# State-space stage of a hybrid backbone on one core: the order inside a tick, the head of the stage, and who adds the two directions of the carried part

## What is computed, cut to what matters

```python
decay = jnp.exp(jnp.where(tri, la[l] - la[s], -jnp.inf))
y_diag = (cc @ bc.T * decay * dt) @ x                # inside the tile
states = bc.T @ (x * to_end)                         # what the tile adds to the state
h = h * chunk_decay + state                          # serial, from tile to tile
y_off = (cc @ h_start) * jnp.exp(la)                 # what was carried in
```

## Time and profile before

| What | us |
|---|---|
| median of 3 runs | 3817.47 |
| the profiled execution, its own time | 3822.76 |
| span of the profiled execution | 3820.9 |
| TensorE busy, share of the span | 88% |
| VectorE busy, share of the span | 63% |
| ScalarE, GpSimd busy, share of the span | 28%, 29% |
| mean granted TensorE clock | 0.953 of 2.4 GHz |

### The profile page before, as it was taken

The page is one execution under the profiler, slowest core; times in us unless marked ns, Lnnn a source line. Parts: engine busy times, 40 slices in busy tenths (PEclk is TensorE's granted clock), DMA queues, the critical chain, the costliest instruction groups (busy, mean ns, idle before and its releaser), DMA issues. The chain is left out here.

```text
span 3820.9 us, 47998 instructions
## 1 busy us (share of the span) xinstructions
PE 3354.3 (88%) x18164; PEld 2734.6 (72%) x18164; DVE 2402.0 (63%) x3949; ACT 1087.8 (28%) x1981; POOL 1093.0 (29%) x794
## 2 busy tenths in 40 slices
PE   6899999999958886886997889999999588958698
PEld 2787888888848785555783577888888488845477
DVE  4134566765448996886564324566875489968765
ACT  2112222212235554332210211222221355523321
POOL 4233334332202232211222423433443022232121
PEclk8999999999979998998998899999999799989899
DMA  5254232223172232344436155322332733133451
GB/s 197 78 150 152 75 98 92 93 87 93 56 216 68 80 96 87 112 114 151 127 99 222 52 114 177 99 85 86 106 96 74 202 92 94 44 110 112 130 152 64
DMA packets 414842, 423.30 MB, mean 111 GB/s; under 512 B 56993, under 2 KB 351393, under 8 KB 413459
## 3 DMA queue, kind: packets, MB, share of 16 engines
q1 hardware_dynamic: 368628, 315.22, 28.6%
q10 hardware_dynamic: 45984, 105.01, 7.8%
HBM read 287.76 MB, written 124.01 MB: 108 GB/s over the span
## 5 line engine op out<-in xcount | busy, mean ns | idle before, releaser
L764 PE MATMUL l_p_acc<-l_u_hi,l_w_hi 128*128 128x512 f32 (+1 forms) x2208 | 606.4, 376 | 26.7 <-ACT l_p_stg L828 12.1
L764 PE MATMUL l_p_acc<-l_u_hi,l_w_lo 128*128 128x512 f32 (+1 forms) x2208 | 588.5, 368 | 0.0
L764 PE MATMUL l_p_acc<-l_u_lo,l_w_hi 128*128 128x512 f32 (+1 forms) x2208 | 587.7, 367 | 0.0
L679 POOL TENSOR_TENSOR l_w_hi<-l_wt,l_p_zero 128x1024 fp32r<-128x1024 f32 x100 | 201.2, 2012 | 914.4 <-PE l_p_acc L764 834.6
L764 PEld LDWEIGHTS l_p_acc<-l_u_hi,l_w_hi 128*128 128x128 f32 x2208 | 384.2, 190 | 104.2 <-issue 30.6
L764 PEld LDWEIGHTS l_p_acc<-l_u_hi,l_w_lo 128*128 128x128 f32 x2208 | 381.2, 189 | 72.0
L764 PEld LDWEIGHTS l_p_acc<-l_u_lo,l_w_hi 128*128 128x128 f32 x2208 | 381.4, 189 | 71.7
L1494 PE MATMUL l_at_pS<-l_at_k_hi,l_at_q 128*128 128x512 f32 (+1 forms) x400 | 166.1, 415 | 125.6 <-ACT l_at_prob L1610 68.9
L1728 DVE TENSOR_REDUCE l_at_nmax<-l_at_pS 128x1 f32<-128x1280 f32 (+1 forms) x144 | 197.2, 1370 | 115.9 <-PE l_at_pS L1495 114.0
L681 POOL TENSOR_TENSOR l_w_lo<-l_wt,l_w_hi 128x1024 fp32r<-128x1024 f32 x100 | 265.8, 2658 | 7.8
L921 DVE TENSOR_TENSOR l_p_R<-l_p_sw,l_p_rs 128x512 f32<-128x512 f32 x72 | 49.6, 689 | 287.4 <-PE l_p_sw L743 287.4
(11 more groups left out here) (361 smaller groups left out, 7264.7 us busy)
## 6 DMA issues: line engine op xcount, KB each, us to landing
l_wt<-w_in SPq DMA_DIRECT2D x104, 512.0 KB, 3.9
l_n_wa<-w_ada SPq DMA_DIRECT2D x10, 2048.0 KB, 17.1
kf_d<-l_p_R SPq DMA_DIRECT2D x72, 256.0 KB, 4.0
xbc_d<-l_p_fin ACTq DMA_DIRECT2D x28, 640.0 KB, 3.0
l_at_K<-kf_d SPq DMA_DIRECT2D x64, 256.0 KB, 3.0
qk_d<-l_p_late ACTq DMA_DIRECT2D x12, 1280.0 KB, 4.6
l_oT<-o_d SPq DMA_DIRECT2D x10, 1024.0 KB, 6.8
l_sd_fed<-xbc_d SPq DMA_DIRECT2D x72, 128.0 KB, 2.5
```

The costliest lines, as they stand in the source:

```text
L679: pool.tensor_tensor(w_hi[m % 2][:], wt[:, m % 2], zero[:].unsqueeze(2).to_broadcast([P, KD, P]), ALU.add).then_inc(w_rounded, 1)
L764: mm = pe.matmul(acc[:, a:a + w], (w_hi, w_lo)[wp][m % 2][:, k], (u_hi, u_lo)[up][:, k, t0 + c:t0 + c + w], start=(k == n == 0), stop=(k = ...
```

## The change

Eight edits, all in `ssd_stage`:

1. In TensorE's tick the carried product comes first, ahead of the first transposes.
2. DVE no longer adds the two directions of the carried part (L2122 goes). TensorE multiplies both with the identity: two L2002 products for each half instead of one.
3. Layer 0, groups 1 to 3: one pair of steps in each of the ticks j = 1 to 9, where j = 1 had two and j = 9 none. Group 0 and layer 1 keep their pairs.
4. Where a tick of groups 1 to 3 still has two pairs (layer 1, j = 1 and j = 7), the second comes after the outputs on TensorE and after the gate on DVE.
5. ScalarE stores output n - 2 at the end of its tick, not at the start.
6. The operands of the exponents have 10 rows instead of 128. POOL sets two rows of one operand only, DVE rounds `sel` once, and one transfer copies it to the eight slots.
7. The first group is loaded in four column ranges, the context, the first and the last two latent tiles, then the rest; ScalarE issues the B rows of each, SP the x rows. The third to sixth tile wait only for their own ranges.
8. The d transfers come after the second group's load, ahead of the pairs 1 and 2, and DVE waits for them at its first gate.

```diff
-    def step_pairs(j):
-        pairs = [0, 1] if j == 1 else [j] if 2 <= j < NSTEP else []
-        if j == NO - 1:
-            pairs = list(range(j, NSTEP))
-        return [2 * k + d for k in pairs for d in range(2)]
+    def step_pairs(g, j):
+        if g and NO > NSTEP:
+            pairs = [j - 1] if j else []
+        else:
+            pairs = [0, 1] if j == 1 else [j] if 2 <= j < NSTEP else []
+            if j == NO - 1:
+                pairs = list(range(j, NSTEP))
+        return [[2 * k + d for d in range(2)] for k in pairs]
+
+    def steps_early(g, j):
+        return step_pairs(g, j)[:1] if g else step_pairs(g, j)
+
+    def steps_late(g, j):
+        return step_pairs(g, j)[1:] if g else []
...
-        seg_l = sb(nc, ctx, tag + "seg_l", [P, RING, 2, P], F32R)
-        seg_r = sb(nc, ctx, tag + "seg_r", [P, RING, 2, HPG, P], F32R)
-        sel = sb(nc, ctx, tag + "sel", [2 + 2 * HPG, HPG, P])
+        SR = 2 + 2 * HPG
+        seg_l = sb(nc, ctx, tag + "seg_l", [SR, RING, 2, P], F32R)
+        seg_r = sb(nc, ctx, tag + "seg_r", [SR, RING, 2, HPG, P], F32R)
+        sel = sb(nc, ctx, tag + "sel", [SR, HPG, P])
+        sel_r = sb(nc, ctx, tag + "sel_r", [SR, HPG, P], F32R)
...
+        first_cols = ((slice(0, CTX), xc_in), (slice(CTX, CTX + 2 * P), xm_in), (slice(T - 2 * P, T), xm_in), (slice(CTX + 2 * P, T - 2 * P), xb_in[0]))
...
-                load_group(0)
-                sp.dma_start(sel[:], sel_d).then_inc(sel_in, 16)
-                for half in range(2):
-                    with nc.allow_non_contiguous_dma(reason="one value per head"):
-                        sp.dma_start(d_s[HD * half:HD * (half + 1), :], skip.rearrange("(n b) -> b n", b=2)[half].partition_broadcast(HD)).then_inc(skip_in, 16)
+                for cols, landed in first_cols:
+                    sp.dma_start(xb[:, 0, 0:XT, cols], xbc_d[0:XG, cols].rearrange("(n p) t -> p n t", p=P)).then_inc(landed, 16)
+                    if landed is xc_in:
+                        sp.dma_start(sel[:], sel_d).then_inc(sel_in, 16)
                 sp.wait_ge(xb_in[0], 32)
+                sp.wait_ge(sel_rounded, 1)
+                sp.dma_start(seg_r[2:SR].bitcast(F32).rearrange("p r d h l -> p (r d) (h l)"),
+                             sel_r[2:SR].bitcast(F32).rearrange("p h l -> p (h l)").unsqueeze(1).to_broadcast([SR - 2, 2 * RING, HPG * P])).then_inc(sel_put, 16)
                 load_pair(0)
                 for n in range(RING):
                     load_decays(n)
                 load_group(1)
+                for half in range(2):
+                    with nc.allow_non_contiguous_dma(reason="one value per head"):
+                        sp.dma_start(d_s[HD * half:HD * (half + 1), :], skip.rearrange("(n b) -> b n", b=2)[half].partition_broadcast(HD)).then_inc(skip_in, 16)
                 load_pair(1)
                 load_pair(2)
...
-                    elif p == (0 if g else CT):
+                    elif g == 0 and p == CT:
+                        pe.wait_ge(xm_in, 64)
+                    elif p == (0 if g else CT + 4):
...
-                        pe.wait_ge(zeroed, 1)
+                        pe.wait_ge(ones, 1)
+                        pe.wait_ge(sel_put, 16)
...
-                        mm = pe.matmul(pY[:, b + t * P:b + (t + 1) * P], us[:, n % 2, 0, 2 * t:2 * t + 2].rearrange("p h e -> p (h e)"), ident[:, :],
-                                       start=False, stop=True)
+                        for d in range(2):
+                            mm = pe.matmul(pY[:, b + t * P:b + (t + 1) * P], us[:, n % 2, d, 2 * t:2 * t + 2].rearrange("p h e -> p (h e)"), ident[:, :],
+                                           start=False, stop=d == 1)
...
+                    if 0 <= n < NO * GROUPS:
+                        carried(n)
                     if todo:
                         prep(g, todo[0], max(n + 1, 0))
                     if ahead:
@@ -2017,18 +2038,23 @@
                     if len(todo) > 1:
                         prep(g, todo[1], 0)
                     preps_done += len(todo)
-                    if 0 <= n < NO * GROUPS:
-                        carried(n)
                     if g < GROUPS:
-                        for k in step_pairs(j):
-                            step(g, k)
+                        for pair in steps_early(g, j):
+                            for k in pair:
+                                step(g, k)
                     if ahead:
                         products(n + 1, preps_done)
                     if 0 <= n < NO * GROUPS:
                         outputs(n)
+                    if g < GROUPS:
+                        for pair in steps_late(g, j):
+                            for k in pair:
+                                step(g, k)
 
...
+                for cols, landed in first_cols:
+                    act.dma_start(xb[:, 0, XT, cols], xbc_d[1024:1024 + P, cols]).then_inc(landed, 16)
...
-                    if 0 <= n - 3 < NO * GROUPS:
-                        store(n - 3)
                     if todo:
                         prep(g, todo[0])
...
                         act.activation(cb[:, n % 2], pC, ACT.Copy).then_inc(cb_copied, 1)
+                    if 0 <= n - 3 < NO * GROUPS:
+                        store(n - 3)
...
-                pool.memset(seg_l[:].bitcast(F32), 1.0).then_inc(ones, 1)
-                pool.memset(seg_r[:].bitcast(F32), 0.0).then_inc(ones, 1)
+                pool.memset(seg_l[0:2].bitcast(F32), 1.0).then_inc(ones, 1)
...
                     dve.tensor_tensor(us[:, n % 2].rearrange("p d h e -> p (d h) e"), pU[:, :].rearrange("p (k e) -> p k e", e=HD),
-                                      decay.unsqueeze(2).to_broadcast([P, 2 * HPG, HD]), ALU.mult).then_inc(u_split, 1)
-                    dve.wait_ge(u_split, n + 1)
-                    dve.tensor_tensor(us[:, n % 2, 0], us[:, n % 2, 0], us[:, n % 2, 1], ALU.add).then_inc(u_scaled, 1)
+                                      decay.unsqueeze(2).to_broadcast([P, 2 * HPG, HD]), ALU.mult).then_inc(u_scaled, 1)
...
+                    else:
+                        dve.wait_ge(skip_in, 32)
...
+                        last = dve.tensor_scalar(mask[:, d, h], tri[:, d], -1.0, 1e30, ALU.add, ALU.mult)
+                last.then_inc(built, 1)
                 dve.wait_ge(sel_in, 16)
+                dve.tensor_copy(sel_r[:], sel[:]).then_inc(sel_rounded, 1)
                 dve.wait_ge(zeroed, 1)
-                dve.wait_ge(ones, 2)
-                for s in range(RING):
-                    for d in range(2):
-                        last = dve.tensor_copy(seg_r[0:2 + 2 * HPG, s, d], sel[:])
-                last.then_inc(built, 1)
-                dve.wait_ge(skip_in, 32)
...
                     if g < GROUPS:
-                        for k in step_pairs(j):
-                            step(g, k)
+                        for pair in steps_early(g, j):
+                            for k in pair:
+                                step(g, k)
                     if 0 <= n - 1 < NO * GROUPS:
                         gate(n - 1)
+                    if g < GROUPS:
+                        for pair in steps_late(g, j):
+                            for k in pair:
+                                step(g, k)
```

More of the change, by code:

```diff
@@ L1847, in ssd_stage @@
+    def steps_early(g, j):
+        return step_pairs(g, j)[:1] if g else step_pairs(g, j)
+    def steps_late(g, j):
+        return step_pairs(g, j)[1:] if g else []
     TICKS = NO * (GROUPS + 1) + 1
     RING, FEDS = 4, 3
-    with stage(nc, tag + "xc_in", tag + "xb0_in", tag + "xb1_in", tag + "o0_in", tag + "o1_in", tag + "o2_in", tag + "seg0_in", tag + "seg1_in", tag + "seg2_in", tag + "seg3_in", tag + "skip_in", tag + "sel_in",
+    with stage(nc, tag + "xc_in", tag + "xm_in", tag + "xb0_in", tag + "xb1_in", tag + "o0_in", tag + "o1_in", tag + "o2_in", tag + "seg0_in", tag + "seg1_in", tag + "seg2_in", tag + "seg3_in", tag + "skip_in", tag + "sel_in", tag + "sel_rounded", tag + "sel_put",
@@ L1852, in ssd_stage @@
                tag + "stored0", tag + "stored1") as (ctx, sems):
-        (xc_in, xb0_in, xb1_in, o0_in, o1_in, o2_in, seg0_in, seg1_in, seg2_in, seg3_in, skip_in, sel_in, zeroed, ones, built, picked, turned, x_copied, end_scaled, state_mm, state_ready,
-         diffed, cb_mm, cb_copied, exped, seg_summed, u_split, u_mm, u_scaled, w_ready, y_mm, skipped, gated, stored0, stored1) = sems
+        (xc_in, xm_in, xb0_in, xb1_in, o0_in, o1_in, o2_in, seg0_in, seg1_in, seg2_in, seg3_in, skip_in, sel_in, sel_rounded, sel_put, zeroed, ones, built, picked, turned, x_copied, end_scaled, state_mm, state_ready,
+         diffed, cb_mm, cb_copied, exped, seg_summed, u_mm, u_scaled, w_ready, y_mm, skipped, gated, stored0, stored1) = sems
@@ L1885, in load_group @@
                         sp.wait_ge(turned, TT * (gr - 1))
-                    for cols, landed in ((slice(0, CTX), xc_in), (slice(CTX, T), xb_in[0])) if gr == 0 else ((slice(0, T), xb_in[gr % 2]),):
```

(4 more changed lines are left out.)

5 lines of the change are left out of this document (1 added, 4 removed).

## The result

The kernel after takes **3852.8 us** (median of 6 runs, 3839.9 to 3860.7) against 3818.7 for the kernel before on the same chip: a ratio of 1.0086 (95% interval 1.0072 to 1.0100), slower by 34 us. The forecast was 3781, with a range that ended at 3800.

A forecast was written before the change was run, and what follows sets the result against it. No engine fills the stage, so the bound was taken to move within a tick. Ticks saving 8.5 and 8.6 us and heads 10.1 and 8.9, together 36.1, took the median 3817.5 to 3781 us, range 3766 to 3800.

The forecast's parts named there:

- Ten rows for 128 in the exponents: Exponent products on TensorE: moving columns stay 512, so no cost counted; bound 7 us either way over 72 outputs.
- Two of the signs: Observations named beforehand as proving the forecast wrong: ticks with preps of 6 us or more, granted clock under 1.00.
- Middle ticks: Ticks with no prep and one pair of steps: 4.45 us plus 0.44 for added products, 4.89, unchanged.
- last group: Ticks without pair or prep: 4.89 less 0.86 us of state products, 4.03.
- second rival: The added identity products on TensorE cost 0.42 us each in all ticks: 3810 us, chance 0.07.
- Prep ticks: Ticks j = 0 to 4: L1979 waits for ScalarE's second copy until 3.46 us, 2.17 follow, sum 5.63.
- first rival: ScalarE's copy is not waited for; prep ticks last 5.4 us with a pair, 4.54 without: 3768 us, chance 0.12.
- Late pair: Layer 1 ticks with a second pair behind the outputs: 6.49 us at j = 1, about 7.2 at j = 7.
- Head: Stage start to first carried product: earlier state operations and carried product save 10.1 us in layer 0, 8.9 in layer 1.
- Moves at no cost: ScalarE's later store, SP's shorter wait, the transfers and ScalarE's added issues: all hidden, no time counted.
- Third rival (GpSimd): In 30 prep ticks VectorE's two-SBUF-input operations wait for GpSimd's: 27 us, up to 3808 us, chance 0.08.
- fourth rival: TensorE's clock falls to 1.2 GHz, some 4.1 us a tick: slower, 3930 us, chance 0.04.

The follow-up runs named there:

- experiment 1: Kernel after with the exponent operands back at 128 rows (10 with data, the rest zeros), all else as changed: 3792.6 us, ratio 0.9921.
- experiment 10: Version 6 with both transposes and their copies ahead of the exponents in ticks with preps and outputs: 3786.5 us, ratio 0.9902.
- experiment 14: Kernel before with the head's edits alone, exponent operands of 128 rows, ticks as before: 3806.9 us, ratio 0.9957.
- version 6: Kernel after with 128-row exponent operands and VectorE adding the two directions again, one identity product per half: 3776.1 us, ratio 0.9877.
- experiment 2: Kernel after, ten rows kept, both exponent products ahead of both mask products, two changes of form a tick, not four: 3827.1 us, ratio 1.0007.

## Why the prediction was wrong

**The step that failed** is "Ten rows for 128 in the exponents: the moving columns stay 512, so I count nothing", with its bound of 7 us either way. Two of the signs that I had named showed it: prep ticks over 6 us (6.54) and a granted clock under 1.00 between the carried products (0.99 and 0.98). Put back, the rows are worth 60 us (experiment 1): four changes of form cost 0.77 us a tick, over the 70 distances 54 us, and the clock gave some 6 more (below). The row closest to it stood in my own working: L2002 ahead of the 64-column L1998 takes 0.42 and ahead of the full-form L1969 0.25, and I named the change of form there. I cited the Trainium skill (TensorEngine Tiling (Array Packing), Key Properties), that a change of tiling mode drains the engine, for the added products alone, and wrote that "the number of drains stays as it is". It doesn't: edit 6 makes four. The Trainium skill (TensorEngine Tiling (Array Packing), Available Configurations) lists modes of 128, 64 and 32 rows. The measured times agree: 10 and 64 rows cost alike, 96 and 128 cost nothing. Applied to edit 6 the rule is a rival of its own: four changes at the 0.17 between those two rows, 72 outputs, 49 us, 3830 us.

**The rest of the sum held**, as experiment 1 shows with edit 6's rows taken out: 3792.6, ratio 0.9921, which from the 3817.5 of the forecast is 3787.3, 6 above it.

- *Middle ticks* 4.89 and *last group* 4.03: both exact. TensorE has no idle time and VectorE has some (13.38 of 14.66 busy in three middle ticks), as said. The added product costs 0.22; the second rival (0.42) falls.
- *Prep ticks* 5.78 instead of 5.63. Experiment 1: first transposes at 1541.70, L1998 (the former L1979) at 1544.31:

```profile
1541.70 0.49 PE L1966 MATMUL l_sd_pT<-ident,l_sd_xb 128*128 128x128 f32 x3
...
1543.28 1.03 PE L1975 MATMUL l_sd_pS<-l_sd_xend,l_sd_tok 128*128 128x256 f32 x4
1544.31 0.46 PE L1998 MATMUL l_sd_pT<-l_sd_fed 128*128 128x128 f32 x2
...
1546.62 0.59 PE L2006 MATMUL l_sd_pU<-l_sd_state,l_sd_fed 128*128 128x512 f32 x1
```

  The chain is 2.61, as forecast; what follows takes 2.31 and not 2.17. With 15 such ticks in layer 0 that is its whole error there (196.42 against 194.1). The first rival falls: ScalarE's second copy ends at 1544.16, just ahead of L1998.
- *Late pair:* 7.27 against 7.2 at j = 7, 6.65 to 6.87 against 6.49 at j = 1. *Layer 1 as a whole* 169.29 against 166.2.
- *Head:* in experiment 1 30.6 and 29.1 us to the first carried product, 8.5 and 8.9 earlier, against 10.1 and 8.9 forecast. In the kernel after it was 10.4 and 4.65; the difference is when the loads land (the second transposes start at 8.6 us in layer 1) and when the clock rises (still 0.50 from 3406 to 3412 us, where layer 0 had 1.00 from 1506 on). The second transposes were forecast at 6.0 us into the stage; they start at 6.5 and 8.6 there, and at 8.2 and 7.3 in experiment 1, where the kernel before had 8.3 and 8.4. So most of what the first state operation gains (17.2 to 11.5 us in experiment 1, layer 0) comes from VectorE's wait for d, which is gone, and not from the earlier columns. Why the loads land at different times was not tried.
- *Moves at no cost:* the store costs nothing, as said.
- *Third rival (GpSimd):* in experiment 1, as in the kernel after, only three of VectorE's weight operations are slow (1.45 us for 0.69), all in the tick after a late pair of layer 1, as I had placed them. The rival falls there. It comes true in part where VectorE adds (experiment 10).

**The fourth rival** (TensorE's clock) came true in part. In the kernel after the clock falls in three places between the carried products, each behind a wait of 0.83 us for ScalarE's copy (in layer 1 with one of 1.35 shortly before): the ticks at 1644.55 and 1652.69 last 8.14 and 8.01 instead of 6.54, and in layer 1 two ticks take 1.4 more. That is some 6 us, not 150. I wrote that gaps of 0.6 to 1.2 in every tick leave the clock at 1.00. The kernel before has ticks with no gap and some with 1.8, and behind one of these its clock does fall (experiment 14). The row at the first place, behind which the stretch from 1650 to 1655 shows 0.50:

```profile
1648.77 0.57 PE L1997 MATMUL l_sd_pT<-l_sd_fed 128*128 128x128 f32 x2 [0.83 <-ACT l_sd_tok L2064]
```

**What the forecast did not ask** is whether edit 2 is still worth having beside edit 1. It said of the middle tick "nothing is won", and in the ticks without a pair it counted 4.03, the wait gone and 0.44 paid. That was right, but 3.58 was to be had there: version 6 is 16 us faster than experiment 1. Of the 16, the ticks show 9.6 (layer 0 188.24 against 196.42, layer 1 167.84 against 169.29) and the heads of the two profiled executions 1.9; the rest I could not place.

Open: why the clock falls behind one wait and not behind another of the same length.

## What to carry to other kernels

In this kernel a TensorE operand of 10 or 64 rows saved nothing and cost 0.2 us at each change of form. Where products of few rows alternate with full ones, count the changes and try padding to the full form first; grouping halved the price only in ticks where no other engine waited for the first result. When two edits remove the same wait, price each alone and both together; one of them may be pure cost. And a price shows in full only when the last idle time has gone, so the edit that removes the waits also exposes what the other edits cost.

## What was not expected of the hardware

- A product of 10 or 64 rows next to one of 128 costs 0.20 us a change (middle ticks 4.89, 5.29 and 5.68 us with no, two and four changes); one of 96 rows nothing (4.91). The weight load (0.18 to 0.19 us) then starts with its product and not 0.23 us ahead.
- Waits of TensorE of 0.8 to 1.8 us were followed in some places by a low stretch (the kernel after shows 0.50, 1.2 GHz, from 1650 to 1655 us; experiment 2 from 1535 to 1545), at a cost of 1.4 to 4.5 us, and in others by nothing, even within one execution.
- Moving ScalarE's copies forward lengthened VectorE's sum of the exponentials, with two SBUF inputs, from 685 to 909 ns in the mean, beside GpSimd's earlier start. The order of the steps alone moves the product with B and C between 692 and 935 ns.
